# The last norm of a two-block transformer kernel: one activation table, gains ahead of the root, residual additions spread over TensorE and GpSimd

## What is computed

```
def second_block(x, ...):
    ...
    h2 = _rmsnorm(x, g_mlp_pre[l])
    ff = jnp.einsum('bsf,fd->bsd',
                    jnp.square(jax.nn.relu(jnp.einsum('bsd,df->bsf', h2, w_up[l]))), w_down[l])
    x = x + _rmsnorm(ff, g_mlp_post[l])

def _rmsnorm(x, g):
    xf = x.astype(jnp.float32)
    r = lax.rsqrt(jnp.mean(xf * xf, axis=-1, keepdims=True) + EPS)
    return (xf * r * g.astype(jnp.float32)).astype(x.dtype)
```

## Time and profile before

| | |
|---|---|
| runs | 2461.8 us median, 2459.86 to 2461.87 (3 runs) |
| profiled execution, from the first to the last instruction (its span) | 2460.0 us; no other time is recorded for it |
| last product of the down projection ends | about 2436.1 us into the span |
| end stage behind it, to the end of the span | about 23.9 us, 1% of the span |
| PE busy | 2419.9 us, 98% |
| DVE busy | 1705.1 us, 69% |
| ACT busy | 1050.4 us, 43% |
| POOL busy | 139.0 us, 6% |
| granted PE clock, mean | 0.997 |

### The profile page before, as it was taken

The page is one execution under the profiler, slowest core; times in us unless marked ns, Lnnn a source line. Parts: engine busy times, 40 slices in busy tenths (PEclk is TensorE's granted clock), DMA queues, the critical chain, the costliest instruction groups (busy, mean ns, idle before and its releaser), DMA issues.

```text
span 2460.0 us, 29760 instructions
## 1 busy us (share of the span) xinstructions
PE 2419.9 (98%) x11494; PEld 1921.0 (78%) x11494; DVE 1705.1 (69%) x2072; ACT 1050.4 (43%) x1495; POOL 139.0 (6%) x227
## 2 busy tenths in 40 slices
PE   8999999999999999999999999999999999999997
PEld 6887755588888888888788777788878888888885
DVE  5237888846877778698873665455588877786888
ACT  5225676624433333333542333343356333334336
POOL 1001100000000010000001000000001000100001
PEclk9999999999999999999999999999999999999999
DMA  5110000132433381600134122233444533715103
GB/s 220 52 43 22 2 1 1 52 137 107 150 119 121 103 307 53 222 1 18 52 100 151 43 78 70 72 133 134 148 150 175 171 103 103 263 45 194 47 1 137
DMA packets 76245, 252.22 MB, mean 103 GB/s; under 512 B 6320, under 2 KB 6368, under 8 KB 76080
## 3 DMA queue, kind: packets, MB, share of 16 engines
q1 hardware_dynamic: 43792, 131.08, 16.7%
q0 software_dynamic: 32320, 119.32, 13.0%
HBM read 186.78 MB, written 62.91 MB: 102 GB/s over the span
## 4 chain that ended last, share of the span: by engine, by line
PE 75%; DVE 10%; issue 4%; ACT 2%; DVEq 0%; ACTq 0%
PE ps L2717 23%; PE ps L3126 20%; PE ps L3164 18%; PE ps L3294 6%; DVE opQ_lo L2132 1%; DVE opQ_lo L2129 1%; DVE spot L2174 1%; DVE ql_raw L2169 1%; DVE Pb L1999 1%; PE ps L3221 1%; PE ps L3240 1%; PE ps L2965 1%; PE ps L3230 1%; PE ps L2839 0%; PE ps L2902 0%
## 5 line engine op out<-in xcount | busy, mean ns | idle before, releaser
L3164 PE MATMUL ps<-opQ_hi 128*128 128x512 f32 x896 | 350.3, 391 | 2.8 <-DVE opQ_lo L2132 2.8
L3164 PE MATMUL ps<-opQ_hi,opQ_lo 128*128 128x512 f32 x896 | 348.7, 389 | 0.0
L3164 PE MATMUL ps<-opQ_lo,opQ_hi 128*128 128x512 f32 x896 | 348.7, 389 | 0.0
L2717 PE MATMUL ps<-opP_hi,w_hi 128*128 128x512 f32 x638 | 199.2, 393 | 2.4 <-DVE w_lo L1620 0.7
L3164 PEld LDWEIGHTS ps<-opQ_hi 128*128 128x128 f32 x896 | 168.2, 188 | 42.1 <-DVE opQ_lo L2132 7.1
L2717 PE MATMUL ps<-opP_lo,w_hi 128*128 128x512 f32 x638 | 196.6, 389 | 0.0
L2717 PE MATMUL ps<-opP_hi,w_lo 128*128 128x512 f32 x638 | 196.4, 389 | 0.0
L3164 PEld LDWEIGHTS ps<-opQ_hi,opQ_lo 128*128 128x128 f32 x896 | 168.2, 188 | 35.1
L3164 PEld LDWEIGHTS ps<-opQ_lo,opQ_hi 128*128 128x128 f32 x896 | 168.2, 188 | 34.7 <-issue 0.2
L1276 ACT ACTIVATE opQ_hi<-spot 128x1024 fp32r<-128x1024 f32 x80 | 84.9, 1062 | 235.9 <-PE ps L3164 196.8
L884 ACT ACTIVATE w_hi<-w_stage 128x1024 fp32r<-128x1024 f32 x104 | 109.4, 1051 | 174.4 <-PE ps L2717 145.4
(11 more groups left out here) (441 smaller groups left out, 4763.0 us busy)
## 6 DMA issues: line engine op xcount, KB each, us to landing
w_stage<-in_w_stream SPq DMA_DIRECT2D x104, 512.0 KB, 3.7
h_spill<-T POOLq DMA_DIRECT2D x56, 512.0 KB, 4.5
pair_raw<-in_w_stream SPq DMA_DIRECT2D x26, 1024.0 KB, 5.8
spot<-in_w_stream SPq DMA_DIRECT2D x24, 1024.0 KB, 7.0
spot<-h_spill POOLq DMA_DIRECT2D x24, 1024.0 KB, 9.5
qh_raw<-in_w_stream SPq DMA_DIRECT2D x8, 1024.0 KB, 11.6
ql_raw<-h_spill POOLq DMA_DIRECT2D x8, 1024.0 KB, 7.5
g_spill<-T POOLq DMA_DIRECT2D x16, 512.0 KB, 2.9
```

The lines of the kernel that those rows point to most:

```text
L2717: mm = pe.matmul(ps[:, psum + half, :], weight, operand[:, k, half * HALF:(half + 1) * HALF], start=(begin and x == 0 and weight is wh and ...
L3164: mm = pe.matmul(ps[:, down_bank(sc, f) + m, :], weight, operand, start=(g == 0 and kt == 0 and weight is wh and operand is hi), stop=(g = ...
```

## The change

On ACT the table for both Ln and Exp is loaded once, by name, ahead of the first of the two last roots, and the later roots use it. The order of ACT's work changes: the last three gains of half 1 come ahead of the squares of the odd tiles of half 0, the first four gains of half 0 come ahead of the second root, and the copies of the pairs from PE come last. DVE scales pair 0 of half 1 ahead of the four last folds. PE adds the residual for three pairs of half 1 (before: two). POOL adds it for pair 3 of half 1 and for pair 0 of half 0 and stores each, then stores the three pairs from PE. DVE keeps the additions of pairs 1, 2 and 3 of half 0 (before: six additions).

```
@@ SP: stores
-            for j in range(3):
-                sp.wait_ge(n4["added"], 2 * DT + 2 + j + 1)
+            for j in range(1, 3):
+                sp.wait_ge(n4["added"], 2 * DT + j)
                 sp.dma_start(out_pair(0, j), end_pair(X, 0, j)).then_inc(y_stored, 16)
             for x in range(2):
-                sp.wait_ge(n4["added"], 2 * DT + 5 + x + 1)
+                sp.wait_ge(n4["added"], 2 * DT + 2 + x + 1)
                 sp.dma_start(out_pair(0, 3)[:, x], end_pair(X, 0, 3)[:, x]).then_inc(y_stored, 16)
-            sp.wait_ge(y_stored, 16 + 16 * 5)
-            sp.wait_ge(ya_stored, 16 * 4)
+            sp.wait_ge(y_stored, 16 + 16 * 4)
+            sp.wait_ge(ya_stored, 16 * 5)
@@ POOL: additions and stores
-            for j in range(2, 4):
-                pool.wait_ge(n4["added"], 2 * DT + j - 1)
-                pool.dma_start(out_pair(1, j), end_pair(X, 1, j)).then_inc(ya_stored, 16)
-            for j in range(2):
+            def added_out(h, j):
+                a, m0 = j // 2, 2 * (j % 2)
+                pool.wait_ge(n4["scaled"], 2 * DT + 4 * (1 - h) + j + 1)
+                for m in range(m0, m0 + 2):
+                    pool.wait_ge(tile_landed[2 * m + a], END_BACK[2 * m + a])
+                link(pool.tensor_tensor(end_pair(X, h, j), end_pair(X, h, j), end_pair(Xend, h, j), ALU.add))
+                pool.dma_start(out_pair(h, j), end_pair(X, h, j)).then_inc(ya_stored, 16)
+
+            def turned_pair(j):
                 pool.wait_ge(n4["ln"], 3 + j + 1)
                 pool.dma_start(out_pair(1, j), end_pair(X, 1, j)).then_inc(ya_stored, 16)
-            pool.wait_ge(ya_stored, 16 * 4)
+
+            added_out(1, 3)
+            added_out(0, 0)
+            for j in range(3):
+                turned_pair(j)
+            pool.wait_ge(ya_stored, 16 * 5)
@@ ACT
             for o in range(4):
                 end_square(0, o)
+            act.preload_act_table_set("natural_log_exp_and_others")
             half_root(n4, 2, 0, end_r[1])
+            for o in range(5, DT):
+                end_gain(1, o)
             for o in range(4, DT):
                 end_square(0, o)
-            for o in range(5, DT):
-                end_gain(1, o)
+            for o in range(4):
+                end_gain(0, o)
             half_root(n5, 2, 1, end_r[0])
-            for o in range(DT):
+            for o in range(4, DT):
                 end_gain(0, o)
-                if o in (1, 5):
-                    pair_out(o // 4)
+            for j in range(3):
+                pair_out(j)
@@ DVE
-                if h == 0 or j >= 2:
+                if h == 0 and j:
@@
+            end_scale(1, 0)
             for o in range(4):
                 last_fold(1, o)
-            for j in range(4):
+            for j in (1, 2, 3):
                 end_scale(1, j)
@@ PE
-            for j in range(2):
+            for j in range(3):
                 a, m0 = j // 2, 2 * (j % 2)
                 pe.wait_ge(n4["scaled"], 2 * DT + j + 1)
+                if j == 1:
+                    pe.wait_ge(ff["down"], vec_no(1, 1, "F4_3"))
```

## The result

The changed kernel takes 2467.51 us (median of 9 runs, 2465.78 to 2468.95) against 2461.61 us for the kernel before (9 runs, 2459.45 to 2462.43): a ratio of 1.0026, 95% interval 1.0017 to 1.0035. The medians differ by 5.9 us, so it is slower. The profiled execution has a span of 2467.0 us against 2460.0. The forecast was a shift of 3.2 us, and a chance of 0.86 that it stays under the 4.9 us (0.2%) that a measurement can tell from nothing. The direction and the queue of stores were right, the size was not.

What follows compares the result with a forecast made beforehand. The end was taken as bound by the chain over DVE and the queue of stores: seven pairs from 2451.45 take 9.7 us, plus 2.14, span 2463.2, 3.2 longer. Median 2461.8 + 3.2 = 2465.0, range 2460.0 to 2468.2.

Steps and rivals of the forecast that it cites:

- the queue of stores: At the end, seven pairs left at 2451.45 keep the DMA engines full for 9.7 us, to 2461.1.
- ACT and the roots: On ACT, one table load at about 2433.3 and half 0's factor ready at 2444.05, against 2445.10 before.
- DVE and POOL wait for each other: Instructions reading two SBUF operands wait whole for each other: 1.6 us lost at scaling (0, 0), 2.1 at addition (0, 1).
- Rival 1: No lock between POOL and DVE: DVE ends at 2452.7, span 2460.7, +0.7 us; chance 0.2.
- DVE's end: With the lock, DVE's last work ends at 2456.3, where it ended before (2456.16).
- Rival 2: Stores are not the bound; a transfer lands 3.3 us after issue whatever the queue; at best -1.4 us; chance 0.12.
- The tail: Behind the last byte at 2461.1 the program takes 2.14 us, as before, giving a span of 2463.2.
- The third pair of PE: Pair 2, copied by 2453.6 and issued at 2453.7, comes into a full queue and costs nothing.
- Rival 3: GpSimd's addition of a pair costs 4.05 us, delaying the full queue: +7.1 us in all; chance 0.1.
- the same: The measured time differs from before by less than 0.2%, 4.9 us; chance 0.86.
- the gain that the change was made of: By ACT and DVE alone, the last addition would end 3.5 us earlier, at 2452.7.

Runs made afterwards that it cites:

- r_psum: The changed kernel with the two last factors written to PSUM and read from there by DVE's scalings; end stage 30.1 us against 30.9, ratio to before 1.0024.
- pool_memset: The changed kernel with each of POOL's two additions replaced by two memsets of the same pair; end stage 29.1 us, 2466.54 us in one run.
- dve_adds: The changed kernel with POOL's two additions back on DVE, POOL only storing; end stage 28.9 us against 30.9, ratio to before 1.0019.

## Why the prediction was right or wrong

- **ACT and the roots: right.** One load at 2433.49, factor 0 at 2444.26. No gap behind the load.
- **DVE and POOL wait for each other: right, and shown.** Forecast was that scaling (0, 0) would get through at 2445.7 and end at 2446.9; it got through when POOL's addition ended, at 2446.00, and ended at 2447.09. The addition of a pair was put at 2.1 and is 2.36; r_psum and pool_memset tie the wait to both engines reading SBUF operands. Rival 1, no lock, is out.
- **DVE's end: right.** Forecast 2456.3, measured 2456.49.
- **The queue of stores: right.** Forecast was a full queue from 2451.45 to 2461.1. It ran from about 2452.05 (a share of 0.00 until 2452) to about 2462.0. Half a microsecond comes from the two longer additions, most of the rest from 366 GB/s where I had 379. That is 0.9 us of the miss. Of the 0.9, 0.2 is that PE's sum starts later. Rival 2 is out: halving the bytes takes 4.5 us away, and POOL's third pair took 7.3 us to land, not 3.3.
- **The tail: this step failed.** The prediction added "the 2.14 behind the last byte" to the last byte's time. That was a difference of two times in one profile, not a mechanism. It took SP's last landing for what ends the program. In fact POOL's last landing did, with a drain of 5.1 us behind it, which before lay mostly beside SP's last stores. In the changed kernel POOL's last landing is within 1 us of SP's, so the drain stands almost whole at the end: 2.8 us more than forecast. The forecast 3.2, the 0.9 and the 2.8 make up, but for rounding, the 7.0 by which the span grew. The row was there to be read before: SP, with all stores landed, waited 1.3 us for the other engines.
- **The third pair of PE: wrong.** "It comes into a full queue and costs nothing" holds for the bytes, but it is POOL's last store, and POOL's last landing is the end. dve_adds shows it: with no lock between the engines (neither waits for the other) the kernel is still 4.8 us behind. The prediction's own sign for this, the third pair as the last store to be issued, missed it: SP's last one was issued later, at 2456.5.
- **Rival 3** had the right size (+7.1 against +7.0 in the profile) for the wrong reason: POOL's row of 3.37 contains the wait for DVE's scaling, as 2.03 did.
- **The range: partly luck.** The median, 2467.51, lies in the stated range of 2460.0 to 2468.2, but 2.5 above the forecast, and only because the range reached up towards rival 3, whose cause is not the one found. The forecast's own limit for "the same", 4.9 us, was passed by the 5.9, an outcome to which it gave 0.11.
- **Two small misreadings** change no sum. POOL's third subtraction ends 0.9 us after QX (249.28 and 248.37), not 1.0. And before 2449 two pairs had left the core (1.05 MB); the third had hardly begun.

So the gain that the change was made of, 3.5 us on ACT and DVE, was lost first to the wait for POOL's reads, then to a queue of stores that was nearly full before. The issue of the last stores moved to the engine whose end is slow, and that added to it: with SP as their issuer 6.1 of the 6.8 us are gone. What stays open is what POOL's drain does in its 5 us; it was seen at 4.9 to 5.1 behind a met wait and at 2.5 to 2.6 behind the landing without one, and no run looked inside.

## What to carry to other kernels

When a stage ends in stores, find what ends the program: follow each issuing engine to its last wait and to what it does behind it, and let the engine with the slow end store first. Before moving work off a chain, check whether the bytes behind it could leave earlier; here the transfers filled 87% of their stretch. GpSimd's additions helped here only while VectorE's instruction had one operand in PSUM, so give GpSimd its share then.

## What the runs showed of the hardware that was not expected

- GpSimd's closing DRAIN, behind a met wait for its own stores, takes 4.89 us where it issued two stores in the end stage, 5.05 where four, 5.13 where five: 0.08 a store. With half of the bytes per store it is 5.13 as well. Without the wait it lasts until 2.5 to 2.6 us after its last store landed. SyncE's takes 0.007 us in every one of these kernels.
- GpSimd's fp32 addition of 128x1024 takes 2.36 us undisturbed; the same addition on VectorE takes 1.22. A VectorE scaling with one operand in PSUM took 1.24 beside it. With two in SBUF VectorE's instruction waited until GpSimd's had ended (1.22 became 2.73, 3.25 and 3.71), and GpSimd's waited likewise (3.37).
- A memset on GpSimd (0.95 us) does not disturb such a VectorE instruction.
- Stores of 512 KB queued one behind the other moved 366 GB/s over ten microseconds (379 over three before); issued into a full queue one took 7.3 us to land, into an empty one 3.2.
